# Crossing the stage boundaries of a two-layer decoder step in two token halves

## The reference

```python
def rmsnorm(x, w): return x * rsqrt(mean(x * x) + EPS) * w
def modulate(h, shift, scale): return h * (1.0 + scale) + shift
def swiglu(h, w_in, w_out):
    gate, up = split(h @ w_in, 2)
    return (silu(gate) * up) @ w_out
for l in range(2):
    mod = silu(c) @ w_mod + b_mod                      # 9 vectors per sequence
    x = x + 0.5 * mod[2] * swiglu(modulate(rmsnorm(x, n0), mod[0], mod[1]), ffn1)
    h = modulate(rmsnorm(x, n1), mod[3], mod[4])
    x = x + mod[5] * (concat[SSD(h), GLA(h), dilated attention(h)] @ w_out)
    x = x + 0.5 * mod[8] * swiglu(modulate(rmsnorm(x, n2), mod[6], mod[7]), ffn2)
y = rmsnorm(x, norm_f)
```

## Time and profile before

| | us |
|---|---|
| median of 3 runs | 2788.12 (2785.95 to 2793.31) |
| the profiled execution | 2792.04 |
| its span, first to last instruction | 2790.3 |
| PE, DVE, ACT busy | 2595.9, 1677.7, 1026.6 |
| mean granted clock of TensorE | 0.938 of full speed |

### The profile page before, as it was taken

The page is one execution under the profiler, slowest core; times in us unless marked ns, Lnnn a source line. Parts: engine busy times, 40 slices in busy tenths (PEclk is TensorE's granted clock), DMA queues, the critical chain, the costliest instruction groups (busy, mean ns, idle before and its releaser), DMA issues. The chain is left out here.

```text
span 2790.3 us, 48559 instructions
## 1 busy us (share of the span) xinstructions
PE 2595.9 (93%) x18959; PEld 2389.0 (86%) x18959; DVE 1677.7 (60%) x2784; ACT 1026.6 (37%) x1607; POOL 12.7 (0%) x43
## 2 busy tenths in 40 slices
PE   5999999799988979999979999979999797999997
PEld 3998998697866779999979999969978567999997
DVE  6872873555743578358468448545366526874864
ACT  3541442312541245235245225323135222542542
POOL 0000000000000000000000000000000000000000
PEclk8999999899995889999989999989899858999999
DMA  7247246312131213643223553552120312232331
GB/s 278 70 122 222 83 117 209 108 54 64 46 105 35 75 46 91 196 144 90 85 59 91 178 161 90 168 175 69 47 64 31 105 53 72 66 97 78 99 87 61
DMA packets 398230, 285.48 MB, mean 102 GB/s; under 512 B 18273, under 2 KB 396439, under 8 KB 397702
## 3 DMA queue, kind: packets, MB, share of 16 engines
q1 hardware_dynamic: 397676, 283.36, 33.6%
q10 hardware_dynamic: 410, 0.18, 0.0%
HBM read 271.71 MB, written 11.79 MB: 102 GB/s over the span
## 5 line engine op out<-in xcount | busy, mean ns | idle before, releaser
L318 PE MATMUL PS<-f_xH,f_wqH 128*128 128x288 f32 x2432 | 713.1, 297 | 50.9 <-DVE f_b12L L1246 44.5
L318 PE MATMUL PS<-f_xL,f_wqH 128*128 128x288 f32 x2432 | 708.4, 296 | 0.0
L318 PE MATMUL PS<-f_xH,f_wqL 128*128 128x288 f32 x2432 | 706.2, 295 | 0.0
L318 PEld LDWEIGHTS PS<-f_xH,f_wqH 128*128 128x128 f32 x2432 | 453.5, 188 | 58.0 <-issue 50.7
L318 PEld LDWEIGHTS PS<-f_xH,f_wqL 128*128 128x128 f32 x2432 | 455.6, 189 | 0.0
L318 PEld LDWEIGHTS PS<-f_xL,f_wqH 128*128 128x128 f32 x2432 | 454.2, 188 | 0.0
L318 PE MATMUL PS<-f_actH,f_wqH 128*128 128x288 f32 x1408 | 308.2, 300 | 0.0
L318 PE MATMUL PS<-f_actL,f_wqH 128*128 128x288 f32 x1408 | 301.1, 295 | 0.0
L318 PE MATMUL PS<-f_actH,f_wqL 128*128 128x288 f32 x1408 | 301.0, 295 | 0.0
L676 DVE SCALAR_TENSOR_TENSOR xT<-PS,modT,xT 128x288 f32<-128x288 f32 (+1 forms) x80 | 41.4, 518 | 412.5 <-PE PS L318 412.5
L318 PEld LDWEIGHTS PS<-f_actH,f_wqH 128*128 128x128 f32 x1408 | 225.3, 189 | 25.0 <-issue 25.0
(11 more groups left out here) (441 smaller groups left out, 4289.8 us busy)
## 6 DMA issues: line engine op xcount, KB each, us to landing
wslot<-in_ffn_w_in SPq DMA_DIRECT2D x176, 512.0 KB, 4.9
masks<-in_w_mod SPq DMA_DIRECT2D x40, 1536.0 KB, 6.7
wslot<-in_ffn_w_out SPq DMA_DIRECT2D x64, 384.0 KB, 4.1
wslot<-in_w_in SPq DMA_DIRECT2D x44, 512.0 KB, 4.7
wslot<-in_ffn_w_out SPq DMA_DIRECT2D x64, 320.0 KB, 3.4
setup<-in_w_mod SPq DMA_DIRECT2D x8, 1536.0 KB, 12.6
wslot<-in_w_out SPq DMA_DIRECT2D x16, 512.0 KB, 4.0
dec<-in_cache_attn_k SPq DMA_DIRECT2D x16, 384.0 KB, 4.0
```

What stands on the lines that cost most here:

```text
L318: ins = e.matmul(outs[j], w, x_hl[j][part], start=(start and w is wh and part == 0), stop=(stop and w is wl), skip_group_check=True)
```

## The change

1. `PLAIN` goes from 2 to 3: one more up unit per feed-forward is computed in the plain way.
2. The last two down tiles (d = 6 and 7) of every feed-forward and of `out_` run half by half: first half of 6, of 7, then second half of 6, of 7. Squares, root and inverse of the first token half are made while PE works on the second halves (`tail_sums`, `tail_act`, `tail_dve`).
3. The weights of the first two units of the next stage are split in that tail, into places of their own (`u0`, `u1`, `in_w`). From setup into the first feed-forward nothing is split ahead: ACT and DVE split both units after the first half's norm tiles.
4. Behind the barrier the norm runs in two halves. PE takes the products of the first half of all tiles first, and the pending rest of tile 7 (`finish_x`) and the second half's root and inverse follow in between.
5. The norm of the first stage is made inside the setup block, and its first two units are loaded there.
6. The final norm and its transposes run in two halves too.

```diff
+        def tail_sums(e, q):
+            e.wait_ge(sem(q + "sq6_added"), 1)
+            e.wait_ge(sem(q + "sq_half"), 2)
+            sum_squares(e, 0, 0).then_inc(sem(q + "tail_sumsq"), 1)
+
+        def tail_act(e, q, opening, rows=lambda: None):
+            e.wait_ge(sem(q + "x_half"), 1)
+            e.wait_ge(sem(q + "sq_added"), DT - 4)
+            square_half(e, DT - 2, 0).then_inc(sem(q + "sq_half"), 1)
+            if opening:
+                next_hi(e, opening[0])
+            e.preload_act_table(ACT.Sqrt)
+            e.wait_ge(sem(q + "x_half"), 2)
+            e.wait_ge(sem(q + "sq_added"), DT - 3)
+            square_half(e, DT - 1, 0).then_inc(sem(q + "sq_half"), 1)
+            e.wait_ge(sem(q + "tail_sumsq"), 1)
+            root(e, 0, 0).then_inc(sem(q + "tail_root"), 1)
+            if opening:
+                next_hi(e, opening[1])
+            rows()
+            e.wait_ge(sem(q + "x_half"), 3)
+            square_half(e, DT - 2, 1).then_inc(sem(q + "sq_half"), 1)
+
+        def tail_dve(e, q, m, banks, first_done, second_done, opening, before=lambda: None):
+            first_done(DT - 2)
+            add_first(e, m, DT - 2, banks[0]).then_inc(sem(q + "x_half"), 1)
+            before()
+            if opening:
+                next_lo(e, opening[0])
+            e.wait_ge(sem(q + "sq_half"), 1)
+            e.wait_ge(sem(q + "sq_added"), DT - 3)
+            add_square_half(e, DT - 2, 0).then_inc(sem(q + "sq6_added"), 1)
+            first_done(DT - 1)
+            add_first(e, m, DT - 1, banks[1]).then_inc(sem(q + "x_half"), 1)
+            e.wait_ge(sem(q + "tail_root"), 1)
+            inverse(e, 0)
+            second_done(DT - 2)
+            link = Link(e, q + "tail_step")
+            add_second(e, link, m, DT - 2, banks[0] + 1, small[:, 0:TS]).then_inc(sem(q + "x_half"), 1)
+            if opening:
+                next_lo(e, opening[1])
+            e.wait_ge(sem(q + "sq_half"), 3)
+            add_square_half(e, DT - 2, 1)
...
-        PLAIN = 2
+        PLAIN = 3
...
+                        for h in range(2):
+                            for n, w in enumerate((u0, u1)):
+                                if h == 0:
+                                    e.wait_ge(w_split, n0 + n + 1)
+                                if n == 1:
+                                    for side in range(2):
+                                        for kt in range(DT):
+                                            ins = plain(w, side, kt, 2 * QW * side, h, 2 + 2 * side + h)
+                                    continue
+                                for kt in range(DT):
+                                    e.wait_ge(sem(q + "h_ready"), kt + 1 if h == 0 else DT + 2 + kt + 1)
+                                    for side in range(2):
+                                        ins = plain(w, side, kt, 2 * QW * side, h, 6 * side + h)
+                                if h == 1:
+                                    ins.then_inc(group_done, 1)
+                                elif pending:
+                                    second_sums(e, q)
...
+                        scaled(0, 0)
+                        for d in range(1, DT):
+                            scaled(d, 0)
+                            low(d - 1, 0)
+                        low(DT - 1, 0)
+                        if pending:
+                            finish_x(e, q, pending, small[:, 0:TS])
+                        else:
+                            next_lo(e, opening_units[0])
+                        sample_scale(e, link, k, s4)
+                        if pending:
+                            second_inverse(e, q)
+                        scaled(0, 1)
+                        sample_rms(e, link, s3)
+                        sample_shift(e, k, s4).then_inc(sem(q + "h_sample"), 1)
+                        scaled(1, 1)
+                        if not pending:
+                            next_lo(e, opening_units[1])
+                        low_samples()
...
+                    e.wait_ge(w_split, u_in + 1)
+                    first_groups(0)
+                    second_sums(e, q)
+                    e.wait_ge(w_split, u_in + 2)
+                    third_group(0)
+                    first_groups(1)
+                    third_group(1).then_inc(group_done, 1)
```

More of the change, by code:

```diff
@@ L76 @@
 MODC = 3
+KH = DT // 2
+QW = KH * P
+XW = KH * HALF
+NWQ = 7 * QW
 CW = 32
@@ L414, in _ @@
                         .then_inc(sem(f"wm_ready{m % 4}"), 16)
+                for n in range(2):
+                    load_unit(e, n)
                 e.wait_ge(sem("masks_made"), 1)
@@ L481, in _ @@
                     keep_mod_rows(e, mrow[:, m, :], 6 + m % 2).then_inc(sem("mrow_ready"), 1)
+                e.wait_ge(sem("sumsq"), 1)
+                e.activation(halves(rms[:]), bank2(2), ACT.Sqrt, scale=1.0 / D, bias=epsc[:]).then_inc(sem("root"), 1)
             @block.tensor
@@ L613, in mod_col @@
             return modT[:, bass.ds(m * DT + d, 1), s:s + n].rearrange("p a s -> p (a s)")
-        def norm_act(e, q):
-            e.wait_ge(sem(q + "sumsq"), 1)
-            e.activation(halves(rms[:]), bank2(0), ACT.Sqrt, scale=1.0 / D, bias=epsc[:])\
-                .then_inc(sem(q + "root"), 1)
-        def norm_pe(e, q):
-            for h in range(2):
-                ins = e.matmul(PS[:, h, 0:HALF], ones[:], halves(rms[:])[:, h, :], start=True, stop=True)
-            ins.then_inc(sem(q + "sumsq"), 1)
@@ L839, in _ @@
                             a, b = up_units(half)
-                            if half == 0 and not prefetched:
-                                load_unit(e, a)
-                                load_unit(e, a + 1)
                             if half == 0:
@@ new lines, in high_samples @@
+                        def high_samples():
+                            e.wait_ge(sem(q + "h_sample"), 1)
+                            for m in range(2):
+                                e.activation(sample_tiles(xH, b12H, m), hf[:, m * KH:(m + 1) * KH, SEQ:T], ACT.Copy)\
+                                    .then_inc(sem(q + "h_hi_samples"), 1)
+                        high(0, 0)
+                        high(1, 0)
+                        for d in range(2, DT):
+                            high(d, 0)
+                            whole(d - 2, 0)
@@ L1066, in _ @@
+                        high(0, 1)
+                        high_samples()
+                        high(1, 1)
+                        for d in range(2, DT):
+                            high(d, 1)
+                            whole(d - 2, 1)
+                        whole(DT - 2, 1)
+                        whole(DT - 1, 1)
                         e.preload_act_table(ACT.Silu)
@@ L1259, in _, with scaled, low @@
-                        lo_gate(n0 + 1, 0, 1)
-                        low(1)
-                        for d in range(4, DT):
-                            scaled(d)
-                            low(d - 2)
-                        low(DT - 2)
-                        low(DT - 1)
+                        s4 = s3.rearrange("p d (b i) -> p d b i", i=NI)
+                        def scaled(d, h):
+                            scale_x(e, k, d, h, hf[:, d, prompt(h)]).then_inc(sem(q + "t_ready"), 1)
+                        def low(d, h):
+                            e.wait_ge(sem(q + "h_hi"), DT * h + d + 1)
+                            out, high = [h_tile(x, b, d, h)[:, 0:prompt(h).stop - prompt(h).start]
+                                         for x, b in ((xL, b12L), (xH, b12H))]
+                            shift_low(e, k, d, out, hf[:, d, prompt(h)], high).then_inc(sem(q + "h_ready"), 1)
@@ new lines, in _ @@
+                        scaled(1, 1)
+                        if not pending:
+                            next_lo(e, opening_units[1])
+                        low_samples()
+                        low(0, 1)
+                        for d in range(2, DT):
+                            scaled(d, 1)
+                            low(d - 1, 1)
+                        low(DT - 1, 1)
+                        lo_gate(n0 + 2, 0, 1)
+                        e.wait_ge(w_hi, n0 + 3)
+                        e.tensor_tensor(wqL[:, 5 * QW:7 * QW], w_raw(n0 + 2)[:, 2 * QW:4 * QW],
+                                        wqH[:, 5 * QW:7 * QW].bitcast(F32), ALU.subtract).then_inc(w_split, 1)
@@ L2795, in _ @@
                                 e.wait_ge(sem("mix_added"), d + 1)
-                                square(e, "out_", sq, d)
-                    for d in range(DT - 4, DT):
+                                square(e, "out_", d)
+                    for d in range(DT - 4, DT - 2):
                         e.wait_ge(sem("mix_added"), d + 1)
-                        square(e, "out_", sq, d)
+                        square(e, "out_", d)
+                    tail_act(e, "out_", ffn_opening(u_ffn2))
                 @block.vector
@@ L2879, in _ @@
```

(8 more changed lines are left out.)

556 lines of the change are left out of this document (337 added, 219 removed).

## The result

The changed kernel takes 2744.71 us (median of 4 runs, 2739.18 to 2751.07) against 2787.36 us before (4 runs), a ratio of 0.9844 (95% interval 0.9813 to 0.9875). Run again on two chips its ratio came out as 0.9812 (0.9784 to 0.9839) and 0.9861 (0.9840 to 0.9882). The forecast was 2736 us, range 2720 to 2762. The profiled execution took 2751.07 us, the slowest of its four; its span is 2749.1 us, 41.2 less than before. The mean granted clock is 0.946.

What follows compares the result with a forecast made beforehand. TensorE, busy 2595.9 of 2790.3 us, was the bound. Boundary gains 22.3 + 13.7 + 21.2 + 6.1 less setup's 6.3 gave 57.0, less 4.5 for clock 52.5: 2792.0 to 2739.5, at the median 2736 us, range 2720 to 2762.

Steps and rivals of the forecast that it cites:

- two signs of being wrong: PE still idling over 8 us at the five inner boundaries, or windows behind them at 0.50 for over 5 us.
- Setup: Setup into first feed-forward: stage starts at 64.7, first product at 76.4 in place of 69.03; ends 6.3 us later.
- Mixer openings: From a mixer's start to its fourth group: 27.0 us in place of 36.5, a gain of 9.5, in two mixers.
- The clock term: Low clock behind new gaps of 2 to 3 us at five boundaries: loses 0 to 7.5 us, taken as 4.5.
- Feed-forward openings: From an inner feed-forward's start to its fourth unit's end: 52.9 us in place of 65.5, a gain of 12.6 each.
- The step of a half: Dependent halves on DVE: 0.40 us each (bounds 0.37 and 0.46), so each further norm tile 0.80 us later.
- Rest of the feed-forwards: Three feed-forwards behind their openings, tails included: 3.3 us less, with loads keeping their places beside the tiles.
- Final norm: Last tail and final norm: stage starts at 14.35 in place of 16.2, end comes at 17.2; gain 6.1 us.
- the third: Low clock lasts until the block products at five boundaries: 100 us slower than before, 2888 us; chance 0.03.
- fourth: Halves don't overlap because a tail waits for loads or the barrier gives time back: 2783, at the median 2779; chance 0.03.
- the second: Clock stays low through the first halves: 5.1 us for eight tiles, five times, 25 us, 2761 us; chance 0.06.
- the first: Chains of dependent halves don't fit their cover: near 4 us in five stages, 20 us, 2756 us; chance 0.10.

Runs made afterwards that it cites:

- the two experiments: Against the changed kernel: setup's turning matmuls ahead of the sum, 2745.39 us; first feed-forward's first unit split ahead of the norm tiles, 2738.72 us.
- new tail order: Changed kernel with the low part of the next stage's first unit moved behind the addition of tile 7's first half in the tails: 2741.84 us, ratio 0.9813.
- the kernel with four edits: Changed kernel plus turning ahead of the sum, first feed-forward's early split, later low part in tails, early modulation load: 2730.67 us, ratio 0.9789.
- the one with the extra matmuls: The kernel with four edits plus unread matmuls at stage starts and in the mixer's 3.1 us gap, none ending out_: 2718.49 us, ratio 0.9737.

## Why the prediction was near, step by step

**The mechanism was right.** Halves hide the second norm, and this is the core of the gain: taking the overlap away alone in three feed-forwards costs 21.6 us of openings. The steps at a boundary came out as forecast: the inverse 1.95 us twice, PE's tail wait 2.19 us in `out_` (forecast 2.3; in the feed-forwards it was 0.57 and 0.38, where 1.3 was forecast), the start of the stages 1.5 and 1.1 us later in `out_` (1.45). The waits for first products came to 26.4 us (13.9, 8.1 and 4.4), a little over the 25 that were named. Of the two signs of being wrong, the idling of over 8 us came at no inner boundary. The other, a clock of 0.50 for more than 5 us, came once in this trace, behind the 3.06 us gap of the second mixer:

```profile
1864.20:1871.00 6.80, 5.73 (x24) 5.73 (x25) 5.82 (x15) 3.20 (x7) 0.00 (x0) 0.50 0.01 2
```

**The number was near in part by luck.** The steps were 19.6 us too favourable. In the profiled pair 8.3 us came from the middles, a term that the forecast didn't have, and the remaining 11.3 are the miss (41.2 in place of 52.5). By terms, for this pair:

- **Setup, 6.1 us.** The turning was put at 7.3 to 9 us and took 10.25, since the clock was 0.50 in all of it, as it is where it stands ahead of the sum (10.41 us). With additions that ended 1.5 us later, the stage starts at 68.3 in place of 64.7. To the first product it took 12.4 us in place of 11.7, from there to the fourth unit's end 53.3 in place of 51.2 (before it was 52.6; the forecast's 52.2 is that of `f2_`). The order itself costs 3 us, the place of the splits 4.2, as the two experiments show.
- **Mixer openings, 6.4 us.** With the clock held, the opening takes 27.4 us, where 27.0 was forecast. All the rest, 2.1 and 3.4 us, is the low clock behind gaps of 2.24 and 3.06 us. The clock term of 4.5 us for all boundaries was meant for this and was too small: it counted one drop per boundary, and a mixer has two.
- **Feed-forward openings, 7.4 us.** At full clock they take 54.6 in place of 52.9. First product 1.78 us after the start (1.45 forecast), a norm tile every 0.86 us (0.80), and 0.132 us per matmul (0.131; a block unit of 84 took 11.11 us between two snapshots already in the earlier trace rows), which is 0.5 us over 372 matmuls. The low clock adds 1.0 and 0.9 in the two `f2_`.
- **The step of a half.** It was read from `TENSOR_TENSOR` rows, starts 0.37 us apart. The norm's `SCALAR_TENSOR_TENSOR` of 288 takes 0.51 us with starts 0.43 apart, as the timeline of DVE in `f1_` layer 1 shows:

```profile
1413.92 0.52 DVE L743 SCALAR_TENSOR_TENSOR f_hf<-xT,modA,rms 128x288 f32<-128x288 f32 x1
1414.35 0.51 DVE L747 SCALAR_TENSOR_TENSOR f_xL<-f_hf,modT,f_xH 128x288 fp32r<-128x288 f32 x1
1414.78 0.51 DVE L743 SCALAR_TENSOR_TENSOR f_hf<-xT,modA,rms 128x288 f32<-128x288 f32 x1
```

The Trainium skill, "VectorE: DVE Perf Modes", in its section on the TRN2 errata, has a fixed cost for every instruction; by its formula, with the cost paid in full, the estimate is 0.91 us a tile. The measured 0.86 lies between this and the forecast of 0.80.
- **Rest of the feed-forwards, 2.1 us.** PE waits 3.7 us for modulation weights in five places. The forecast said that loads keep their places; they did, but PE waits for this load at the first down units. The second trace of the kernel before has 2.4 us of the same waits in three places, and against it the rests fall by 2.4 to 4.5 us, around the forecast 3.3. So this term is within the scatter.
- **Final norm, 2.5 us.** PE waits 2.50 us for the second halves behind the first transposes, which the forecast hid behind two copies.

**Rivals.** Nothing speaks for the third and fourth; the second happened in part (low clock at the front of most openings, never for all eight tiles at 1.44 us); the first had the right places and too high prices for each (a feed-forward opening at full clock was 1.7 us over the forecast, where it had 4), though its sum of 20 us is about what the steps fell short by.

**Left open.** The kernel before has middles of 435 to 441 us in two traces (mean 437.3) and the changed one 428 to 437 in three; over all 12 traces of the changed kernel and its variants the mean is 431.5 (425.0 to 439.6), while the medians of all runs ask for about 5 us per middle. PE's matmuls in them are the same, and its waits sum to 31.4 to 33.7 us in every one, while the granted clock of a middle goes from 0.868 in the longest to 0.900 in the shortest. So the clock makes the difference; why it was lower before isn't shown.

## What to carry to other kernels

When a stage boundary is a chain on VectorE, let TensorE start on the part of the data that is ready, and then look at every wait that is left in the new order: an instruction of 2.3 us that stands in front of a short one on which TensorE waits costs most of its length (1.8 us here), and where TensorE itself sets the boundary it costs only the wait. A gap of 2 to 3 us costs more than itself if the clock falls behind it; a few matmuls without use close it, and where a wait some 9 us ahead of it was removed, the clock held too. Before single microseconds are compared, cut the traces at fixed marks, take more than one trace of each kernel, and find the stretches that scatter.

## What the runs showed of the hardware

The same gap can keep or lose the clock. Behind 2.24 us of idling the first products of `f1_` layer 1 ran at 2.4 GHz in two traces and lost 0.9 us in a third; in the five other kernels that keep this 2.24 us gap and the overlap behind it, it was lost each time (openings of 55.4 to 55.5 us). In front of `f2_` the gap in the kernels with the overlap and without extra matmuls is 2.75 to 3.14 us. Where PE had also waited 2.19 us in the tail, some 9 us earlier, the opening lost about 0.9 us in 12 of 12 cases; where that wait was 0.35 us (new tail order, alone and with the other edits), the clock stayed at 1.00 in 4 of 4. With PE busy in the gap no opening of the two kernels that do this was longer than at full clock (54.6 to 54.8 and 27.4 us, ten openings).

In one long stretch the clock differs with the same work. The two windows of each pair are of the decode part, layer 0, in the kernel with four edits (middle 425.1 us), then in the one with the extra matmuls (437.5 us):

```profile
855.00:895.00 40.00, 39.16 (x257) 30.49 (x258) 10.43 (x32) 8.43 (x21) 0.00 (x0) 0.61 0.20 60
895.00:935.00 40.00, 33.16 (x181) 26.04 (x180) 25.37 (x33) 11.32 (x16) 0.00 (x0) 0.75 0.24 77
```

```profile
853.00:893.00 40.00, 39.16 (x227) 29.15 (x225) 5.75 (x17) 5.73 (x15) 0.00 (x0) 0.50 0.13 40
893.00:933.00 40.00, 33.16 (x134) 23.90 (x133) 20.00 (x43) 12.20 (x18) 0.00 (x0) 0.56 0.24 72
```

By the records PE is busy for 39.16 of 40 us in the first window of both, and the granted clock is 0.61 in one and 0.50 in the other. Most matmuls there have 8 or 16 columns, and their records overlap, so this share says little of what the array did. The Trainium skill, "TensorE: Matmul & The Clock Gate", part 1, says that the clock goes by how busy the engine has been; the openings of the kernels with extra matmuls agree (1.00 in each), and this stretch can't decide it. The middles, in which no kernel was edited, scatter by 8.5 us in the traces of the changed kernel and by 14.6 over all 12, and decide most of the difference between two runs.
